# Expert rows scaled on VectorE and summed on TensorE by accumulating transposes, in place of products with a diagonal matrix

## The reference, cut to what matters

```
qv = (xi @ wq).reshape(B, PEER_BLOCK, PEER_HEADS, 2, half)
...
expert = jnp.take_along_axis(cand_i, best_j, axis=-1)
gate = jax.nn.softmax(best_s, axis=-1)
act = jax.nn.gelu(jnp.einsum('btd,bthkd->bthk', xi, u_tab[expert]).astype(jnp.float32), approximate=False)
return jnp.einsum('bthk,bthkd->btd', (gate * act).astype(xi.dtype), v_tab[expert])
```

## Time and profile before

| | |
|---|---|
| median of 3 runs | 2938.54 us (2937.18 to 2946.53) |
| profiled execution, first to last instruction | 2942.0 us |
| PE busy, of the span | 2618.3 us, 89% |
| DVE busy | 1387.1 us, 47% |
| ACT busy | 925.3 us, 31% |
| POOL busy | 679.5 us, 23% |
| HBM traffic | 836 MB read, 285 GB/s over the span |
| mean granted TensorE clock | 0.959 of full speed |

### The profile page before, as it was taken

How to read it: one execution, slowest core, us unless ns; L and a number is a source line. 1 busy time by engine, 2 the same in 40 slices (tenths; PEclk the granted TensorE clock), 3 DMA queues, 4 the chain that set the end, 5 groups by cost and what they waited for, 6 DMA issues and landing times.

```text
span 2942.0 us, 30348 instructions
## 1 busy us (share of the span) xinstructions
PE 2618.3 (89%) x11408; PEld 1770.9 (60%) x11408; DVE 1387.1 (47%) x3167; ACT 925.3 (31%) x2331; POOL 679.5 (23%) x615
## 2 busy tenths in 40 slices
PE   7878998979999999999898899999799999877786
PEld 6757887856875878655443666555376655343222
DVE  3574333341002233564656564545755554676444
ACT  1551112110000220354623244532334552333332
POOL 0010112110000000232333223333322322433332
PEclk9988999989999999998999998999999999999999
DMA  6221121123344568998899898999998999998997
GB/s 255 86 88 58 58 79 44 72 79 143 143 155 159 226 248 322 387 420 339 325 408 397 337 419 335 420 411 421 378 371 368 370 380 422 399 374 339 422 422 328
DMA packets 109987, 839.09 MB, mean 285 GB/s; under 512 B 12177, under 2 KB 12433, under 8 KB 13969
## 3 DMA queue, kind: packets, MB, share of 16 engines
q0 software_dynamic: 73728, 536.90, 45.2%
q1 hardware_dynamic: 36112, 300.25, 25.9%
HBM read 836.06 MB, written 1.05 MB: 285 GB/s over the span
## 4 chain that ended last, share of the span: by engine, by line
PE 62%; DMA 15%; DVE 12%; ACT 8%; issue 2%; POOL 1%; SPq 0%; DVEq 0%; POOLq 0%; ACTq 0%
PE psm L2141 16%; DMA mem<-in_puv,mem 13%; PE psm L430 10%; PE psm L1711 6%; PE psm L438 5%; DVE mem L2185 3%; PE psm L717 3%; PE psm L2016 3%; PE psm L1349 3%; PE psm L1246 3%; PE psm L1903 2%; PE psm L1397 1%; DMA mem<-in_pwq 1%; PE psm L434 1%; PE psm L732 1%
## 5 line engine op out<-in xcount | busy, mean ns | idle before, releaser
L2141 PE MATMUL psm<-mem 128*128 128x512 f32 x2048 | 1017.6, 626 | 157.9 <-ACT mem L2159 153.2
L2169 POOL DMA_INDIRECT mem<-in_puv,mem x512 | 563.0, 1100 | 1209.6 <-PE psm L2141 1141.6
L2185 DVE CUSTOM_DVE_ANT_0 mem<-mem 128x1024 f32<-128x1024 f32 x512 | 624.0, 1223 | 419.4 <-DMA mem<-in_puv,mem 418.6
L2141 PEld LDWEIGHTS psm<-mem 128*128 128x128 f32 x2048 | 373.7, 196 | 609.1 <-ACT mem L2159 300.4
L430 PE MATMUL psm<-mem 128*128 128x256 f32 (+2 forms) x1504 | 349.8, 395 | 34.1 <-DVE mem L1179 15.7
L430 PEld LDWEIGHTS psm<-mem 128*128 128x128 f32 x1504 | 291.2, 196 | 92.0 <-issue 32.1
L2153 ACT ACTIVATE mem<-mem 128x1 f32<-128x1 f32 x512 | 102.5, 200 | 675.6 <-DVE mem L2185 674.6
L1711 PE MATMUL psm<-mem 128*128 128x256 f32 x1024 | 240.0, 386 | 0.5 <-ACT mem L1425 0.5
L1711 PEld LDWEIGHTS psm<-mem 128*128 128x128 f32 x1024 | 197.2, 194 | 56.7 <-issue 31.4
L2159 ACT ACTIVATE mem<-mem 128x128 f32<-128x128 f32 x512 | 206.0, 402 | 16.9
L438 PE MATMUL psm<-mem 128*128 128x128 f32 x1408 | 190.3, 279 | 19.4 <-ACT mem L985 5.9
(11 more groups left out here) (355 smaller groups left out, 2379.0 us busy)
## 6 DMA issues: line engine op xcount, KB each, us to landing
mem<-in_w2g SPq DMA_DIRECT2D x64, 1024.0 KB, 7.9
mem<-in_w SPq DMA_DIRECT2D x18, 2048.0 KB, 8.3
mem<-in_pwq SPq DMA_DIRECT2D x32, 1024.0 KB, 10.8
mem<-in_w2f SPq DMA_DIRECT2D x28, 1024.0 KB, 9.0
mem<-in_wgu SPq DMA_DIRECT2D x11, 2048.0 KB, 7.6
mem<-in_w2t SPq DMA_DIRECT2D x20, 1024.0 KB, 10.9
mem<-in_w2b SPq DMA_DIRECT2D x16, 1024.0 KB, 9.6
mem<-in_w2o SPq DMA_DIRECT2D x16, 1024.0 KB, 9.9
```

Of the source, the lines that this page charges most:

```text
L2141: m = pe.matmul(bank(6 + h), DG[:, n % 4, :], GR[n % PING][:, 1024 + h * 512:1536 + h * 512], start=k == 0, stop=k == 127)
L2169: po.indirect_dma_start(GR[n % PING], None, A[f"puv{i // 2}"], bass.IndirectOffsetOnAxis(ap=IX[i % 2][:, k:k + 1], axis=0)).then_inc(gsem[ ...
L2185: ve.tensor_tensor_reduce(out=GR[n % PING][:, 0:1024], in0=GR[n % PING][:, 0:1024], in1=X[:, i % 2, :], scale=1.0, scalar=0.0, op0=MUL, op ...
```

## The change

DVE scales the `v` half of the gathered slot in place, by the gelu and by the gate as two per-token scalars (`expert_scale`), one expert behind its dots: after dot n comes the scaling of expert n-1. ACT keeps only the gelu. PE no longer multiplies by a diagonal matrix: it transposes the eight 128x128 pieces of the scaled `v` half with the identity and lets them accumulate in the same two banks, so that the sum over the experts stands there transposed. `fin` therefore first copies both banks to SBUF (`YT`, half by DVE, half by ACT), transposes them back on PE into banks 6 and 7, and goes on as before. `fin` has two more steps in the plan, and four of them are placed between the first and second expert step of the next tile. The wait that frees a slot for the next gather is still that for PE's last instruction of the expert.

```diff
-        DG = at(place(512), 4, 128)
+        YT = at(place(1024), 8, 128)
...
+            placed_at += [(128.0 * i + 1.1 + 0.1 * k, ("fin", i - 1)) for k in range(4) if i >= 1]
+            lane = [("fin", i - 1)] * 8 * (i >= 1) + [(s, i + 1) for s in (tile_steps(i + 1) if i < 3 else [])]
...
-        plan += [("e", NE), ("e", NE + 1)] + [("fin", 3)] * 10
+        plan += [("e", NE), ("e", NE + 1)] + [("fin", 3)] * 12
...
 def expert_pe(pe):
...
-                pe.wait_ge(*EA[n])
-                for h in R2:
-                    m = pe.matmul(bank(6 + h), DG[:, n % 4, :], GR[n % PING][:, 1024 + h * 512:1536 + h * 512], start=k == 0, stop=k == 127)
+                pe.wait_ge(*EV["v", n])
+                for c in R8:
+                    m = pe.matmul(bank(6 + c // 4)[:, tsl(c % 4)], GR[n % PING][:, 1024 + c * 128:1152 + c * 128], ident, is_transpose=True,
+                                  start=k == 0 and c % 4 == 0, stop=k == 127, skip_group_check=True)
                 m.then_inc(EP.next(n), 1)
...
 def expert_ac(ac):
...
-                co, g = CO[i % 2][:, k:k + 1], GT_[i % 2][:, k:k + 1]
-                if k % 32 == 0:
-                    ac.wait_ge(*TV[i, k // 32, "gt"])
-                ac.wait_ge(*EV[n])
-                ac.activation(co, DO[i % 2][:, k:k + 1], ACT.Gelu).then_inc(oa.up(), 1)
-                ac.wait_ge(*oa.now())
-                ac.activation(co, co, ACT.Copy, scale=g).then_inc(oa.up(), 1)
-                ac.wait_ge(*oa.now())
-                if n >= 4:
-                    ac.wait_ge(*EP[n - 4])
-                ac.activation(DG[:, n % 4, :], ident, ACT.Copy, scale=co).then_inc(EA.next(n), 1)
+                ac.wait_ge(*EV["d", n])
+                ac.activation(CO[i % 2][:, k:k + 1], DO[i % 2][:, k:k + 1], ACT.Gelu).then_inc(EA.next(n), 1)
...
 def expert_ve(ve):
...
-                                        op0=MUL, op1=ADD, accum_out=DO[i % 2][:, k:k + 1]).then_inc(EV.next(n), 1)
-                yield
-            yield
-            yield
+                                        op0=MUL, op1=ADD, accum_out=DO[i % 2][:, k:k + 1]).then_inc(EV.next(("d", n)), 1)
+                if n:
+                    expert_scale(ve, n - 1)
+                yield
+            expert_scale(ve, NE - 1)
+            yield
+            yield
+
+        def expert_scale(ve, n):
+            i, k = n // 128, n % 128
+            v = GR[n % PING][:, 1024:2048]
+            if k % 32 == 0:
+                ve.wait_ge(*TV[i, k // 32, "gt"])
+            ve.wait_ge(*EA[n])
+            ve.tensor_scalar(v, v, CO[i % 2][:, k:k + 1], GT_[i % 2][:, k:k + 1], MUL, MUL).then_inc(EV.next(("v", n)), 1)
...
 def fin_ve(ve, i):
...
             ve.wait_ge(*EP[128 * i + 127])
+            ve.tensor_copy(YT[:, 0:4, :], by(bank(6), 128)).then_inc(PV.next((i, "y")), 1)
+            yield
+            yield
             for h in R2:
                 xx = x[:, h * 512:h * 512 + 512]
+                ve.wait_ge(*PP[i, f"y{h}"])
                 ve.scalar_tensor_tensor(xx, xx, al, bank(6 + h), MUL, ADD).then_inc(PV.next((i, f"x{h}")), 1)
...
 def fin_pe(pe, i):
+            yield
+            for c in R2:
+                pe.wait_ge(*(PV[i, "y"] if c == 0 else PA[i, "y"]))
+                for k in R4:
+                    m = turn(pe, bank(6 + c)[:, tsl(k)], YT[:, 4 * c + k, :])
+                m.then_inc(PP.next((i, f"y{c}")), 1)
+            yield
...
 def fin_ac(ac, i):
-            for _ in range(9):
+            ac.wait_ge(*EP[128 * i + 127])
+            ac.activation(YT[:, 4:8, :], by(bank(7), 128), ACT.Copy).then_inc(PA.next((i, "y")), 1)
+            for _ in range(11):
                 yield
```

More of the change, by code:

```diff
@@ L264, in build @@
             placed_at = [(128.0 * i + k, ("e", 128 * i + k)) for k in range(128)]
-            lane = [("fin", i - 1)] * 10 * (i >= 1) + [(s, i + 1) for s in (tile_steps(i + 1) if i < 3 else [])]
+            placed_at += [(128.0 * i + 1.1 + 0.1 * k, ("fin", i - 1)) for k in range(4) if i >= 1]
+            lane = [("fin", i - 1)] * 8 * (i >= 1) + [(s, i + 1) for s in (tile_steps(i + 1) if i < 3 else [])]
             total, done = sum(weight[s] for s, _ in lane), 0.0
@@ L284, in build @@
                     mix=[("b", n, 2 * n + 2, 2 * n + 3) for n in R4] + [("o", n, 12 + n, 12 + (n | 1)) for n in R4] + [("ga", 0, 19, 21)],
-                    query=[("q", n, 4 * n, 8 * (n // 2) + 7) for n in R8], fin=[("gf", 0, 6, 7)])
+                    query=[("q", n, 4 * n, 8 * (n // 2) + 7) for n in R8], fin=[("gf", 0, 8, 9)])
         step, nth2, last2 = {}, {}, {}
@@ L405, in build @@
         TV = marks("t_v", [(i, c, x) for i in RI for c in R4 for x in ("ix", "g3", "gt")])
[L406 to L409, removed]
+        EP, EA = [marks(n, range(NE)) for n in ("e_p", "e_a")]
+        EV = marks("e_v", [x for n in range(NE) for x in [("d", n)] + [("v", n - 1)] * (n > 0)] + [("v", NE - 1)])
+        PP = marks("p_p", [x for i in RI for x in [(i, "y0"), (i, "y1")] + [(i, c) for c in R2 if i < 2]])
+        PV = marks("p_v", [(i, x) for i in RI for x in ["y", "x0", "x1", "st", "l"] + ["h"] * (i < 2)])
+        PA = marks("p_a", [x for i in RI for x in [(i, "y")] + [(i, "h")] * (i < 2)])
         PO = marks("p_o", RI)
@@ L1339, in fm_pe @@
                 pe.wait_ge(*PV[i - 2, "h"])
-                pe.wait_ge(*PA[i - 2])
+                pe.wait_ge(*PA[i - 2, "h"])
             for n in range(7):
@@ L2229, in fin_po @@
             v = ln_parts(i % 2)[2]
-            for _ in range(4):
+            for _ in R6:
                 yield
@@ L2253, in fin_ac @@
                 ac.wait_ge(*PP[i, 1])
-                ac.activation(HT[:, 4:8, tsl(i % 2)], by(bank(1), 128), ACT.Copy).then_inc(PA.next(i), 1)
+                ac.activation(HT[:, 4:8, tsl(i % 2)], by(bank(1), 128), ACT.Copy).then_inc(PA.next((i, "h")), 1)
             yield
```

## The result

The changed kernel took 2986.01 us (median; 2982.28 to 2986.21) beside 2941.78 us for the kernel before (2937.18 to 2946.53): a ratio of 1.0142, 95% interval 1.0123 to 1.0162. It is slower by 44 us where 35 us less were forecast; the difference of 1.4% is small but clear of the interval. The profiled execution has a span of 2984.3 us at a mean granted clock of 0.865 (0.959 before).

A forecast was written before the change was run, and what follows sets the result against it. TensorE and transfers were taken to trade the lead from 1200 to 2700 us, gathers alone to bound it after. Bound -24, waits -18 and tile finishes +7 gave -35 us: 2904 us in the median, range 2840 to 2990.

The forecast's parts named there:

- The added wait: Slot loop: scaling waits one more landing; last-tile hold 6.0 us, 6.9 with slow transposes, period still 2.48 us.
- a fifth taken off the waits: Expert stage, 1200 to 2700 us: of 88 us in which engines wait for each other, 18 us were to go.
- the 34 us of VectorE per piece: Scaling's added VectorE load in each 150 us piece of the stage, at 0.81 us each; 339 us in the 1500.
- The largest of three: Per 150 us piece, the largest of TensorE busy, VectorE busy and transfers at 419 GB/s; sum falls 1412 to 1388 us.
- The end: After the last dot: added copies, transposes and scaling were to cost 1 to 3 us, taken as 2.
- The dense routing of tile 3: Last piece of the stage: 18 us worse, as VectorE takes the lead at 143 of 150 us.
- The first tile's dense routing: First two pieces of the stage: 144.3 us before and after in the first, 134.6 to 123.4 in the second.
- The transposes were taken at 1.06 us: TensorE, per expert: eight transposes at the low price replace 1.99 us of products, giving back 0.93 us.
- B: Rival: VectorE becomes the bound if over 86% of its 321 us of other waits survive; 2991 us, chance 0.20.
- C: Rival: TensorE's clock falls, transposes run at 1.97 us and TensorE keeps its load; about 2965 us, chance 0.11.
- A: Rival: transfers set the whole expert stage, at 405 GB/s or more; 2862 us, 2814 at the floor, chance 0.15.
- D: Rival: an even trade, TensorE's freed time is waited out on VectorE; 2930 to 2947 us, chance 0.12.

The follow-up runs named there:

- half width: The changed kernel scaling 512 of 1024 columns: 2942.9 us; beside it, the changed kernel without scaling plus a 512-column scratch multiplication nobody waits for: 2902.2 us.
- 768 unlinked columns: The changed kernel without scaling, plus a VectorE multiplication of 768 scratch columns behind each dot that no other engine touches: 2911.7 us (0.9891).
- ordinary products: The changed kernel with four of eight pieces per expert (first and last of a tile excepted), as non-transposing products with the identity: 2994.2 us (1.0185).
- the two zero products: The changed kernel with two products by a zero matrix ahead of TensorE's wait for each scaling, except a tile's first expert: 2998.7 us (1.0195).

## Why the prediction was wrong

**The step that failed** is "The added wait": the wait of the scaling was priced in the slot loop of the last tile, where it fits, and in the mixed stage only by the words that "the scaling now waits with them", with a fifth taken off the waits all the same. What the runs put in its place, as shares of the time of before (2941 us), since runs of different groups are compared:

- TensorE's relief: the run without scaling stands at 0.9776, -66 us. The prediction's sum without the 34 us of VectorE per piece would be 1367 - 1412 = -45, -18 and +7, together -56. So the TensorE side was sized about right, though not by the load: TensorE gave back half of what was counted on (below). With half of it taken off in each piece the bound would be the same 1367, since the transfers hold it in every piece.
- VectorE's load: +25 us for 280 us, +34 us for 350 us. Carried on along this line to 415 us it is +42 us; this value is an estimate, since the full width was not run unlinked in this kernel, and the ratios that it rests on are good to 0.2%, 6 us, each. The largest of three charged 1388 - 1367 = 21 us. It lets load cost nothing until VectorE leads a piece.
- The link: what is left of the 108 us, some 66, an estimate too (43 measured at half width). The prediction had nothing for it outside the last tile.

Together -66 + 42 + 66 = +42, the measured ratio of 1.0142; it must come out so, because the last term is the remainder. The miss of 77 us is then the link, 66, and load priced at half of what it cost, 21, less 10 us of gain more than forecast.

**The other steps.** The scaling costs 812 ns (0.81 forecast). The slot is held 5.87 us where the transposes take 1.09 (6.0 forecast), 6.6 as the mean of dots 420 to 499, most of which have slow transposes (6.9 forecast for these), and the last tile keeps its period. The end costs 2.8 us (1 to 3), with some luck: two scalings and sixteen transposes stand behind the last dot where one and eight were counted, 4.3 us in place of 2.3 to 3.2, and the finish adds 1.5 in place of 1.75 to 2.66. The dense routing of tile 3 was to get worse by 18 us and lost 15, or 19 counted from dot 368. The number fits better than its reason: VectorE is at 128 of 150 us there, not over 90%, and waits for the rest, and with 768 unlinked columns the same 32 dots lose 4 us, so a good part of the 15 is the link, which the sum didn't have. The first tile's dense routing, which the sum saw as transfer-bound in its first piece (144.3 before and after) and gaining in the second, lost 11.

The transposes were taken at 1.06 us per expert and average 1.41 (722.4 us over 512), because groups of 1.06 to 1.10 and of 1.8 to 1.97 us alternate with the clock. In the 140 us of the last tile above, 9 of the 56 groups took 1.1 us and the others 1.7 to 2.0. The rest of TensorE's busy time rose too, from 1600.7 to 1669.8 us, some 8 of it the new finish. TensorE gave back 226 us in all where 476 had been counted on; from 1200 to 2700 us it is 75% busy, over the 62 to 70% forecast. That it hardly mattered is seen in the run without scaling, with 76% and 66 us gained.

**The rivals.** *B* ended nearest in time (2991) and had the right engine and the right tie, "through it to TensorE's bursts, which the dot never waited for". But its condition was wrong. Of the 321 us of other waits 144 survived, 45%, far below the 86% from which it was to decide, and a new one of 73 us came in, the link, which B had named but not priced. B's time came near because another error cancels this one: it added up as if all 293 us of gather waits could be filled, and 133 of them stayed. VectorE never became a full engine; its two expert lines hold 21% of the chain, as much as the gathers. *C*: the clock fell, to 0.84 in the stage, just under the mark of 0.85 that the prediction had set for it, and to 0.61 in the last tile. But the kernels without scaling and with scaling on ScalarE have 0.88 as a mean, and gain 66 and 30 us; the low clock doesn't stop the gain. What it costs by itself is open. The reason given for C doesn't hold either. The Trainium skill, "TensorE: Matmul & The Clock Gate", Part 4, says that transposes don't count as busy in the way other matmuls do. The traces don't agree: in the same 140 us 448 instructions of ordinary products got 0.63 and 444 transposes 0.61. TensorE ran nothing but transposes in this stretch, and the clock still rose at times, as 0.61 is above 0.5 and a group of 1.09 us stands at 2864.16 above. With 221 small instructions added to the transposes it was 1.00. *A* needs 405 GB/s; even without scaling it was 400. *D* held in the middle tiles, where gain and price cancelled (13.4 us late at dot 32, 19.0 at dot 368), and nowhere else.

## What to carry to other kernels

Work moved to an engine that is "only 60% busy" isn't free when that engine is an in-order part of a loop of slots: unlinked work cost 0.09 to 0.16 us per us here, and work that waits for another engine and has a third one waiting for it cost 0.26 (0.24 at half width). Price a new wait in every stage, not in the one where the loop is easiest to read, and put the operation where the wait stands behind nothing, even if it takes 42% longer there. Before adding idle time to an engine's room, ask whether its wait would move with the work: VectorE's gather waits were filled by about half.

## What the runs showed of the hardware

The busy share by itself doesn't tell the granted clock: in the last tile it was 1.00 at 79% busy in the kernel before and at 65% with the two zero products, and 0.61 at 71% in the changed kernel, where the eight transposes themselves had stretched from 1.06 us to 1.8 (444 of them in 99.5 us of the row above). A busy share read at the low clock overstates the work: over the whole kernel the same 4096 transposes were busy for 722 us at a mean clock of 0.865 and for 591 us at 0.951, with the zero products. A multiplication of 128x1024 float32 by two columns takes 812 ns on VectorE (545 for 512 columns, 683 for 768), and the one-column form 1150 on ScalarE.
